# The order of the expert weights in the load queue: down weights directly behind their own gate and up weights

## The reference

```
pg = softmax(t @ rg + rgb);  p_top, g_idx = top_k(pg, 1)          # one group of 4
le_g = (t @ re + reb) of that group;  q, e_idx = top_k(softmax(le_g), 2)   # two experts of 8
h = silu(einsum('nd,edf->nef', t, wg)) * einsum('nd,edf->nef', t, wu)
h = h * comb[:, :, None]                                          # weights of the choice
y = einsum('nef,efd->nd', h, wd)
...
y_prompt, y_sample = rmsnorm(x + y, final_norm)
```

## Time and profile before

| | us |
|---|---|
| median of 3 runs (lowest, highest) | 859.47 (858.55, 863.85) |
| the profiled execution's own time | 859.35 |
| its span, first to last instruction | 857.5 |
| TensorE busy | 789.5 (92%) |
| VectorE busy | 449.4 (52%) |
| ScalarE busy | 249.4 (29%) |
| GpSimd busy | 68.0 (8%) |
| expert weights in the trace, issued by SP | 96 MiB of 159.86 MB moved in all |

### The profile page before, as it was taken

One profiled execution on the slowest core, in us unless ns is written; L12 is line 12 of the kernel. 1 busy time (PEld: TensorE's weight loads), 2 busy tenths in 40 slices (PEclk: granted clock), 3 DMA queues, 4 the chain that ended last, 5 costly groups with the idle time before them and its releaser, 6 DMA issues.

```text
span 857.5 us, 16408 instructions
## 1 busy us (share of the span) xinstructions
PE 789.5 (92%) x6202; PEld 496.0 (58%) x6202; DVE 449.4 (52%) x1085; ACT 249.4 (29%) x587; POOL 68.0 (8%) x78
## 2 busy tenths in 40 slices
PE   4999999999999999999999999998899998888780
PEld 4666666666666666666666665455555554444440
DVE  2376587686786786886885946235212121111124
ACT  4223352451451442432423533121111111111121
POOL 3000000000000000000000000001322322222110
PEclk9999999999999999999999999999999999999995
DMA  9552160160250150330510461868999999999975
GB/s 218 125 136 50 25 174 15 27 179 7 60 150 24 39 146 24 90 96 24 146 40 24 146 253 39 330 263 336 321 383 378 389 384 386 397 391 385 389 278 189
DMA packets 116403, 159.86 MB, mean 186 GB/s; under 512 B 27855, under 2 KB 91905, under 8 KB 109432
## 3 DMA queue, kind: packets, MB, share of 16 engines
q1 hardware_dynamic: 100260, 149.14, 51.5%
q0 software_dynamic: 5328, 6.08, 2.4%
q10 hardware_dynamic: 10773, 4.06, 1.9%
HBM read 156.00 MB, written 13.64 MB: 198 GB/s over the span
## 4 chain that ended last, share of the span: by engine, by line
PE 64%; DVE 13%; SPq 13%; DMA 4%; issue 3%; ACT 1%; DVEq 1%; POOL 0%; ACTq 0%; POOLq 0%
PE bank L708 18%; PE bank L1100 7%; SPq L486 5%; PE bank L878 5%; PE bank L997 4%; PE bank L1107 4%; SPq L515 3%; PE bank L816 3%; SPq L489 3%; PE bank L714 2%; PE bank L823 2%; DMA vecs<-in_exp_up 2%; PE bank L1093 2%; PE bank L680 2%; DVE vecs L1629 2%
## 5 line engine op out<-in xcount | busy, mean ns | idle before, releaser
L708 PE MATMUL bank<-xnT,wall 128*128 128x320 f32 x656 | 198.2, 444 | 3.0 <-DVE wkv L1666 1.7
L708 PEld LDWEIGHTS bank<-xnT,wall 128*128 128x128 f32 x656 | 118.0, 189 | 52.0 <-DVE wkv L1666 4.8
L1944 DVE SCALAR_TENSOR_TENSOR vecs<-vecs,bank 128x128 f32<-128x128 f32 x32 | 9.2, 287 | 138.0 <-ACT vecs L1457 138.0
L1100 PE MATMUL bank<-vecs,scratch 128*64 128x256 f32 x384 | 45.8, 393 | 9.2 <-DMA vecs<-in_exp_up 8.3
L1940 DVE COPY vecs<-bank 128x512 f32<-128x512 f32 x32 | 22.1, 691 | 58.9 <-PE bank L1107 41.1
L603 POOL DMA_INDIRECT merged<-xn2d,gidx x4 | 3.7, 920 | 589.3 <-DVE gidx L1922 588.4
L1457 ACT ACTIVATE vecs<-bank 128x128 f32<-128x128 f32 x32 | 8.9, 277 | 129.0 <-PE bank L1100 129.0
L878 PE MATMUL bank<-xnT,wall 128*128 128x320 f32 x128 | 43.9, 455 | 0.3
L1217 ACT ACTIVATE shared<-bank 128x256 f32<-128x256 f32 x32 | 12.3, 385 | 109.5 <-PE bank L708 103.6
L1100 PE MATMUL bank<-scratch 128*64 128x256 f32 x320 | 36.7, 382 | 6.7 <-DMA scratch<-in_exp_up 5.5
L1100 PEld LDWEIGHTS bank<-vecs,scratch 128*64 128x64 f32 x384 | 27.7, 141 | 23.6 <-DMA vecs<-in_exp_up 9.5
(11 more groups left out here) (378 smaller groups left out, 1378.2 us busy)
## 6 DMA issues: line engine op xcount, KB each, us to landing
wall<-in_w_in SPq DMA_DIRECT2D x58, 512.0 KB, 5.7
vecs<-in_exp_gate SPq DMA_DIRECT2D x12, 1024.0 KB
vecs<-in_exp_up SPq DMA_DIRECT2D x12, 1024.0 KB
scratch<-in_exp_gate SPq DMA_DIRECT2D x10, 1024.0 KB
scratch<-in_exp_up SPq DMA_DIRECT2D x10, 1024.0 KB
scratch<-in_exp_down SPq DMA_DIRECT2D x6, 1024.0 KB
wall<-in_exp_down SPq DMA_DIRECT2D x6, 1024.0 KB
shared<-in_exp_gate SPq DMA_DIRECT2D x10, 512.0 KB
```

What stands on the lines that cost most here:

```text
L708: q = mm(tpbank(L, name), wbuf[name][:, k, :], xnT[:, k, :], start=(k == 0), stop=(k == KC - 1))
L1100: q = mm(b[64 * f:64 * f + 64, 0:256], xT[:, k, :], gate_up(w, k)[:, :, 128 * f:128 * f + 128], start=(k == 0), stop=(k == KC - 1))
```

## The change

The calls of `next_gu` and `next_dn` are put in another order. No transfer, buffer, semaphore or size is changed.

```
@@ -542,14 +542,10 @@
                 sp.wait_ge(S("dn"), e - 5)
                 load_dn(e % 6, e)
 
-            next_gu(6)
-            next_gu(7)
-            next_dn(6)
-            next_dn(7)
-            next_gu(8)
-            for e in range(9, NE):
+            for e in range(6, NE - 1):
                 next_gu(e)
-                next_dn(e - 1)
+                next_dn(e)
+            next_gu(NE - 1)
             next_dn(NE - 1)
             sp.wait_ge(S("gu"), 28)
```

## The result

The changed kernel takes 861.94 us (median of 20 runs, 860.23 to 866.69), the kernel before 858.77 (20 runs, 857.25 to 864.15). The ratio is 1.0034, with a 95% interval of 1.0021 to 1.0048: slower by 2.9 us (1.8 to 4.1); the two medians themselves differ by 3.2. The forecast was 2.8 us more and 862.3 us in all. It started from a time before of 859.47 us, 0.7 above the one measured here, so a part of its closeness in the total is luck: the effect was forecast a little too small and the start a little too high.

The account below looks back on a forecast made before the run. The prediction took the stream of expert weights through never-idle DMA engines as the bound. 859.35 us plus 2.8 for one MiB, others 0, gave 862.15; with 0.12 for the median, 862.3 us, 8 in 10 within 859.5 to 866.0.

Parts of the forecast that it names:

- What bounds: Expert stage, second half: the DMA stream of weights sets the pace, and expert 31's up weights fix the end.
- The term: End of SP's queue: down 30 ahead of gate 31 puts 1 MiB more before `up(31)`, 2.8 us later.
- rival 1: End of the queue: order in the rings doesn't matter, up 31 arrives as before, 859.4 us; 12%.
- It exists once, not per expert: Middle of the expert stage: the 2.8 us delay comes once; experts stay 8.57 us apart.
- SP's late issues cost nothing: From gate 7 on: issues 3.8 or 3.3 us late are hidden by transfers already issued; 0 us, range 0 to 3.8.
- the case that the cover is gone: Late issues of gate 7 to 11 starve the rings: 3.8 us for one place, 13.7 for four; 8%.
- rival 2: At 600 to 616 us, holding gate 7 back lets gathers run alone, winning up to 3.6 us, 858.6; 5%.
- rival 4: At `up(31)`: TensorE falls to its lower clock after a wait, 1.7 us more, 864.0 us; 7%.

Follow-up runs that it names:

- the double dose: Kernel before, but down 30 and down 31 both loaded ahead of gate and up 31; 867.23 us, ratio 1.0104.
- the sixth experiment: Kernel before, with every load from expert 6 on waiting for one finished expert more; 861.69 us, ratio 1.0030.
- the second experiment: Changed kernel, but the end loaded as before: gate and up 30, gate and up 31, down 30, down 31; 860.31 us, ratio 1.0018.
- first experiment: Kernel before with only the last pair exchanged: down 30 loaded ahead of gate and up 31; 865.30 us, ratio 1.0083.
- fourth experiment: Kernel before with only the last pair exchanged, plus 13 unused matmuls ahead of `up(31)` to keep TensorE busy; 862.14 us, ratio 1.0046.
- experiments 7 and 8: Kernel before, twice, with 1 MiB of down 4 and 5 issued earlier to fill a DMA gap; 859.13 and 858.80 us, ratios 1.0004 and 1.0005.

## Why the prediction was right, point by point

**What bounds.** Right, and shown from three sides. A MiB added ahead of `up(31)` costs 2.7 us of distance, two cost 5.5, and one taken away in the middle of the stream gives 3.0 back. The term was 2.8, and the change shows 2.86. The distance from `up(18)` to `up(30)`, which was to stay near 102.8 us, is 102.95.

**The order in the rings doesn't matter (rival 1).** Refuted by the change itself, whose `up(31)` waits for an arrival 2.86 us later, and by the double dose, which moved it by twice as much as one MiB.

**It exists once, not per expert.** Right. `up(30)` is 231.25 us behind `up(0)` in the changed kernel against 228.57, 2.7 more, and `up(31)` 2.9 more. TensorE's first wait for weights comes at `up(16)`, at 705.43, where before it came at `up(17)`: its stock ended one product earlier, as said, and nothing more was added from there to the end.

**SP's late issues cost nothing.** Right: a share of 1.02 and more, and a kernel with them but with the old end that lies within 0.7 us in distance. The price for the case that the cover is gone was too high, though. The prediction had 3.8 us for one place and 13.7 for four, one us for each us of delay. In the sixth experiment a delay of 11 us at gate 7 and those behind it cost 2.7 in all. What failed there, in the rival and not in the sum, is to set a late issue equal to idle engines. SP's own waits weren't gone behind 623 either: from 635 to 820 us of the kernel before it waited 11.0 us for finished `up`, in five waits. But they cost nothing, at a share of 1.02 and more, so the prediction was right not to count them.

**Faster by gathers that run alone (rival 2).** Not borne out. With gate 7 held back and the old end, the kernel was not below before. The rate in the 16 us where the gathers run was 312 GB/s in the changed kernel and 329 in the second experiment, against 303 before, 0.1 and 0.4 MB more, which is 0.4 and 1.1 us at most. The kernels of the two filled gaps, with the old order, show 310 and 294 there, so it isn't shown that even this comes from the order.

**TensorE's clock (rival 4).** The mechanism is real, and the prediction was right that it would not strike here: the wait before `up(31)` is 1.48 us. The reason it gave was thin. All seven profiles with a wait of 1.29 to 1.56 us ahead of `up(31)` show 3.67 us for it. What keeps the wait short in the changed kernel is that `up(30)` is late by the same MiB, and that delay had been taken long before: `up(16)`, `up(17)` and `up(18)` start 1.8, 2.6 and 2.6 us later relative to `up(0)` than before, and no wait behind them is longer than 2.0 us, as before. Where only the last pair is exchanged, the whole MiB falls into one wait of 4.14 us, and the clock adds 2.3 us (3.2 by the medians of the first and fourth experiment).

**What stays open.** The first experiment measured 6.6 us by medians and its profile accounts for 5.1, the double dose 8.5 against 7.0. Both accounts lie within the intervals, so the rest may be noise. It may also be the clock: had `up(31)` run wholly at the lower one, it would have taken twice 3.67 us, 1.3 more than the 6.00 shown and 2.2 more than the 5.19 (an estimate from these rows). No profile of the other executions exists.

## What to carry to other kernels

Where a stream of loads sets the end, order it by when each load is consumed, and count the bytes that stand ahead of the last product: a MiB that is needed only behind that product costs its full transfer time if it stands ahead of it. A late issue costs what the DMA engines in fact fail to move (0.9 MB and 2.7 us for issues 11 us late), so look at their share and their bytes, not at the time of issue. Before you compare the stretches of two profiles, move them so that they hold the same part of the program. Moving one load at the very end can cost more than moving all of them: it put the whole MiB into one wait of 4.14 us ahead of the last long product, which then ran at the lower clock.

## What the runs showed of the hardware that was not expected

- In the stretch of hand to mouth, four products of the changed kernel took 5.36 us instead of 3.67 after waits of 1.82 to 1.93 us, others took 3.67 after waits up to 2.00. So the length of the last wait alone doesn't decide it; in the double dose `up(2)` took 5.36 us behind an idle time of only 0.73. In the stretch of hand to mouth it cost nothing, since TensorE then waited less for the next weights (0.23, 0.27, none and 0.19 us):

```profile
722.80 5.36 PE L1096 MATMUL bank<-vecs,scratch 128*64 128x256 f32 x32 [1.82 <-DMA vecs<-in_exp_up]
...
766.37 3.67 PE L1096 MATMUL bank<-shared,scratch 128*64 128x256 f32 x32 [2.00 <-DMA shared<-in_exp_up]
```

- Two short stretches at the lower clock in the first 40 us of the profiled execution cost it 3.7 us at the start of the expert stage, with the same program ahead of it: two groups of products took 10.57 and 6.18 us instead of 8.88 and 4.49. It isn't tied to this change: the profiled executions of experiments 7 and 8, which don't have it, and of experiment 2 began the stage as late (594.05 to 594.52), those of the other five and the kernel before at 590.36 to 591.24. What brings the clock down there in some executions isn't known. That is more than the effect of the change, and a comparison of whole spans of two profiles would have shown 7.3 us where the kernels differ by 2.9.
